# Branch B's scores as two split matmuls from stacked operands, with B's key block moved ahead of its query block, in a two-layer attention encoder

## The chip, the cores and the metric

One NeuronCore of one Trainium2 chip runs the whole program. The metric is the device time in microseconds (us) of one execution, lower is better. The engines that matter are TensorE (PE in the profile, its weight loads PEld), VectorE (DVE), ScalarE (ACT) and the DMA queues that SyncE (SP) and ACT issue on.

## The reference

Two layers over 512 tokens of width 1024. Each layer normalises x, projects it once, feeds four token mixers (A: windowed attention, B: differential attention, C: dilated, D: latent), gates and adds their outputs, projects, and runs a gated MLP. Branch B is the one changed most:

```python
def differential_attention(b_q, b_k, b_v, pos, q_norm, k_norm, ..., subln_g, lam_init):
    q = rms_norm(b_q.reshape(b, s, 2, B_HEADS, HEAD_DIM), q_norm)   # 2 maps x 4 heads x 64
    k = rms_norm(b_k.reshape(b, s, 2, B_HEADS, HEAD_DIM), k_norm)
    v = b_v.reshape(b, s, B_HEADS, B_V_DIM)                         # 4 heads x 128
    def block(args):                                                # 128 queries at a time
        sc = jnp.einsum('bqmhd,bsmhd->bmhqs', qblk, k) * scale
        sc = sc - slopes * dist
        a = jax.nn.softmax(sc, axis=-1)
        a = a[:, 0] - lam[None, :, None, None] * a[:, 1]            # two maps mixed
        return jnp.einsum('bhqs,bshv->bqhv', a, v)
```

## The kernel before

**Dense work.** Every projection is a series of "visits". A visit is six matmuls of 128x512 into one of PSUM banks 0 to 3: each fp32 operand is held as a rounded high part and a low part, and high x high, low x high and high x low are added up (`split3`, line 579). A weight tile comes by DMA into `raw`, ACT writes its high part `wh` (L961), DVE its low part `wl` (L1481, called "the split" below); one tile serves four visits.

**Order.** The engines' queues are written by generators that yield a due number, counted in visits; `together` merges them. So each engine has one fixed order, and semaphores do the rest. `ORDER` lists the dense blocks; `WINDOW` says over which visits the attention of a branch is spread. A window is cut into slots, one score each: B has 32 scores, 36 slots, over 45 visits (blocks br0a, gate0b, br0b and gate1a).

**A slot of B on TensorE.** A score is one matmul of `q_pad` (a head's 64 query rows, the other 64 rows zero) with `kT`, 512 keys, both plain fp32, into the single bank S1 (L859). DVE adds the distance bias while it copies the bank out (L2017), ACT takes the exponential (L1366). For every pair of scores (the two maps of a head) DVE mixes the two (L2007, L2009, L2011), TensorE transposes the mix (four matmuls on L614 into bank TA, "the turn"), ACT and DVE copy halves of it to SBUF (L1360, L2023), and TensorE multiplies it with the values (four matmuls, L850). The next score may not start before the bias has emptied S1 (`s_biased`). In its queue the mix of a pair stands ahead of the bias of the score after the pair, the turn stands one slot behind that, the values another two.

**Stacks of A.** Branch A already takes its scores from stacked operands: `q_two` holds query high parts over all 128 rows for a first matmul and low parts for a second, `kA` holds key high parts in 64 rows and key low parts in the other 64, and two matmuls of the rounded fp32 type (fp32r) make one score (L815). ACT writes the high parts (L1324), DVE copies them to the other 64 rows and subtracts for the low parts (L1955, L1957), for eight pieces of two halves each.

**Branch outputs.** Blocks br0a and br0b end in four merges on DVE each (L1621 and L1624), which multiply a bank by its gate and add it up. L1878 writes the low part of a turned tile of A's or D's output.

Of the kernel before, what the change touches and what calls it, by code (L numbers as in the profile page):

```python
# [13 lines left out]
F32 = mybir.dt.float32  # L14
F32R = mybir.dt.float32r
# [6 lines left out]
P = 128  # L22
# [87 lines left out]
class Own:  # L110
# [5 lines left out]
    def done(self, layer):  # L116
# [7 lines left out]
    nt_dve=24, ta_ready=128, ta_act=128, ta_dve=128, q_padded=48, q_hi=16, q_stacked=16, q_zeroed=2, s_ready=144, s_biased=144, p_ready=144, b_mixed=16, o_ready=128, o_out=24,  # L124
    gains_in=1, ssum=16, lam_dot=1, lam_exp=1, c_diff=2, c_exp=2, merged_sum=24, merged_hi=8, merged_lo=8, conv_mid=44,
    e_ready=22, hidden_val=22, hidden_hi=22, hidden_lo=22, act_step=189, dve_step=534, params_in=16, direct_in=8,
# [44 lines left out]
PADS = dict(C0=16, C1=8, C2=8, B=16)  # L171
# [31 lines left out]
def slots(name):  # L203

    begin, end, n = WINDOW[name]
    return [(step, begin + (end - begin) * step / (n + 4), (end - begin) / (n + 4)) for step in range(n + 4)]
# [24 lines left out]
def _build(nc, io, ctx):  # L231
# [20 lines left out]
    near = sb("near", [P, 2, NEAR])  # L252
    bias_b = sb("bias_b", [P, TT, SEQ])
    bias_c12 = sb("bias_c12", [P, 2, SEQ])
# [36 lines left out]
    q_two = stacked[:, AD + 4096:AD + 6144].rearrange("p (c h s n) -> p c h s n", c=4, h=2, s=2)  # L291
    gates = in_work(AD + 6144, 2048, t=4)
# [27 lines left out]
    c0_stats = nc.dram_tensor("c0_stats", (2, SEQ, 8), F32).ap()  # L320
    gate_keep = nc.dram_tensor("gate_keep", (2, P, 4 * SEQ), F32).ap()
# [31 lines left out]
    q_zeroed = signal("q_zeroed")  # L353
    s_ready = signal("s_ready")
# [35 lines left out]
    pad_clear = sem("pad_clear")  # L390

# [152 lines left out]
    def _(pe):  # L544
# [3 lines left out]
        def layer(l):  # L548
# [145 lines left out]
            def dense():  # L694
# [20 lines left out]
                for part in "qkv":  # L715
                    yield from block(f"B{part}", 4, tokens_out(H), pj_act)
# [28 lines left out]
            def turns():  # L745
# [26 lines left out]
                yield from head_turns(END["Aq"] + 6, chunks_of(stage))  # L772
                yield from head_turns(END["Bq"] + 6, chunks_of(stage))
                yield from head_turns(END["Bk"] + 6, chunks_of(stage))
# [51 lines left out]
            def attention_b(scores_of, begun):  # L826
# [5 lines left out]
                for step, at, pace in slots("B"):  # L832
                    yield at
                    if 3 <= step < n + 3 and step % 2 == 1:
                        pair = (step - 3) // 2
                        pe.wait_ge(*b_mixed.at(l, pair + 1))
                        pe.wait_ge(*ta_act.at(l, n_att[0]))
                        pe.wait_ge(*ta_dve.at(l, n_att[0]))
                        n_att[0] += 1
                        group[pair] = n_att[0]  # L840
                        transposed(TA, [mixed[:, pair % 2, P * k:P * k + P] for k in range(4)], ta_ready)
                    if 5 <= step < n + 5 and step % 2 == 1:
                        pair = (step - 5) // 2
# [7 lines left out]
                        last.then_inc(*o_ready.up())  # L851
                    if step < n:
# [3 lines left out]
                        pe.wait_ge(*q_padded.at(l, n_pad[0] + pads_of("B", step)))  # L856
                        pe.wait_ge(*s_biased.at(l, first + step))
                        for out, st, mv, start, stop in scores_of(step, S1):
                            mm(out, st, mv, start=start, stop=stop).then_inc(*s_ready.up())  # L859
# [11 lines left out]
            def attentions():  # L871
# [40 lines left out]
                yield from attention_b(b_scores, heads_in(B_HEADS, 96))  # L912
# [7 lines left out]
    def _(act):  # L920
# [47 lines left out]
        def layer(l):  # L968
# [107 lines left out]
            def dense():  # L1076
# [30 lines left out]
                n_dve[0] += 8  # L1107
                yield from staged_squares("Bq", 512)
                yield from staged_squares("Bk", 512)
                yield END["Bk"] + 2  # L1110
# [80 lines left out]
            def turns():  # L1191
# [49 lines left out]
                yield from q_out(END["Aq"] + 6, qA, 0)  # L1241
                yield from q_out(END["Bq"] + 6, qT, 4)
                yield from k_out(END["Bk"] + 6, kT, "bk")
# [42 lines left out]
            def pads():  # L1286
# [22 lines left out]
                def stacks_of_a():  # L1309
                    first, slot = done, slots("A")  # L1310
                    for piece in range(8):
# [9 lines left out]
                        for half in range(2):  # L1321
                            mine = slice(64 * half, 64 * half + 64)
# [18 lines left out]
                by_pair, by_map = (lambda g: slice(2 * g, 2 * g + 2)), (lambda g: slice(g, 4, 2))  # L1341
# [6 lines left out]
                yield from tiles_of("B", qT, B_HEADS, by_map)  # L1348

            def attention_b():  # L1350
# [3 lines left out]
                for step, at, pace in slots("B"):  # L1354
                    if 3 <= step < n + 3 and step % 2 == 1:
                        yield at + 0.05 * pace
                        pair = (step - 3) // 2
# [19 lines left out]
            def attentions():  # L1377
# [15 lines left out]
                yield from attention("C2", subs=4, mins=7, sums=10)  # L1393
                yield from attention("D", tile_at=0)
# [5 lines left out]
                act.dma_start(x_sb, keep).then_inc(*x_moved.up())  # L1400

# [6 lines left out]
    def _(dve):  # L1408
# [74 lines left out]
        def layer(l):  # L1483
# [220 lines left out]
            def dense():  # L1704
# [92 lines left out]
                yield from branch_out("br3b", 1, GATES, loaded=3)  # L1797
                yield from head_norm("Bq")
                yield from head_norm("Bk")
# [80 lines left out]
            def turns():  # L1880
# [42 lines left out]
                yield from q_out(END["Aq"] + 6, qA, 0)  # L1923
                yield from q_out(END["Bq"] + 6, qT, 4)
                yield from k_out(END["Bk"] + 6, kT, "bk")
# [18 lines left out]
            def stacks():  # L1944

                slot, n = slots("A"), 0
                for piece in range(8):
                    t, g = piece // 2, piece % 2
                    yield (slot[4 * piece - 4][1] + 0.8 * slot[0][2] if piece >= 2 else slot[0][1] - 6 + 1.5 * piece) + 0.3
                    for half in range(2):  # L1950
                        n += 1
# [6 lines left out]
                                        q_two[mine, 2 * g:2 * g + 2, half, 0, :].bitcast(F32), ALU.subtract).then_inc(*q_stacked.up(own))  # L1958

# [35 lines left out]
            def attention_b():  # L1995
# [3 lines left out]
                for step, at, pace in slots("B"):  # L1999
                    if 2 <= step < n + 2 and step % 2 == 0:  # L2000
                        yield at + 0.02 * pace
                        u = step - 2
# [9 lines left out]
                    if step < n:  # L2012
                        yield at + 0.2 * pace
                        dve.wait_ge(*s_ready.at(l, first + step + 1))
                        dve.wait_ge(*p_ready.at(l, first + step - 1))
                        dve.sem_inc(waits_met, 1)
                        v.tensor_tensor_reduce(out=scores[:, step % 2, :], in0=S1[:, :], in1=bias_b[:, step // 8, :], scale=B_SLOPES[(step % 8) // 2], scalar=MASKED, accum_out=stat[:, 5, step:step + 1], op0=ALU.add, op1=ALU.min).then_inc(*s_biased.up(own))  # L2017
                    if 3 <= step < n + 3 and step % 2 == 1:
                        yield at + 0.4 * pace
                        pair = (step - 3) // 2  # L2020
# [3 lines left out]
                    if step >= 11 and (step - 11) % 8 == 0:  # L2024
                        yield at + 0.6 * pace
                        t = (step - 11) // 8
# [7 lines left out]
            def attentions():  # L2034
# [42 lines left out]

                yield from attention("C0", biased_near(1, C_SLOPES[0], mins=12), keep_c0, 8, keys=near_keys)
# [7 lines left out]
            return norm1(), dense(), turns(), stacks(), attentions(), c_combine()  # L2086
# [31 lines left out]
```

## Time and profile before

| what | value |
|---|---|
| median of 3 runs (lowest, highest) | 2702.33 us (2701.27, 2704.14) |
| profiled execution, its time | 2702.53 us |
| its span, first to last instruction | 2700.7 us |
| PE busy | 2628.6 us (97%) |
| DVE busy | 1637.8 us (61%) |
| ACT busy | 1231.9 us (46%) |
| mean granted TensorE clock | 0.997 of 2.4 GHz |

The time of an execution is 1.8 us above its span. PE busy time is the union of matmul records whose ends are modelled, so what a matmul costs is read from the distance between starts. DVE's 61% is a mean over stages that differ a lot.

### The profile page before, as it was taken

To read this page: it belongs to the slowest core of one execution; us is meant where nothing else is said; L and a number is where in the kernel's file an instruction comes from. 1 tells how busy PE (TensorE), PEld (TensorE's weight loads), DVE (VectorE), ACT (ScalarE), POOL (GpSimd) and SP (SyncE) were. 2 spreads that over 40 slices of the span, in tenths; PEclk is the share of its full clock that TensorE was granted. 3 is DMA by queue.
4 is the path that set the end of the run, shared out by engine and by line. 5 is a ranking of instruction groups with operands and counts; after the bars stand their busy time and mean duration, and the time that the engine had idled before them with its cause. 6 is when DMAs were issued, how large, how long until landed. Compare 5 with 4: busy or idle time off the path is not lost. (4 is left out here: it accounts for less than half of the span.)

```text
span 2700.7 us, 36172 instructions
## 1 busy us (share of the span) xinstructions
PE 2628.6 (97%) x12982; PEld 2207.3 (82%) x12982; DVE 1637.8 (61%) x3432; ACT 1231.9 (46%) x2514; POOL 1.5 (0%) x6
## 2 busy tenths in 40 slices
PE   7999999999999999999999999999999999999999
PEld 6999987777877778888779998877788777888887
DVE  6554577545666647666664546775356666585665
ACT  5655554444544334333355455544446443343332
POOL 0000000000000000000000000000000000000000
PEclk9999999999999999999999999999999999999999
DMA  5212222222121323332342122221221213333332
GB/s 185 71 56 79 81 65 86 63 71 79 56 78 49 110 94 92 94 103 87 102 122 67 49 85 75 78 86 55 71 79 55 79 47 110 94 94 101 95 101 94
DMA packets 143874, 225.28 MB, mean 83 GB/s; under 512 B 15046, under 2 KB 69458, under 8 KB 142802
## 3 DMA queue, kind: packets, MB, share of 16 engines
q1 hardware_dynamic: 135842, 201.85, 25.1%
q10 hardware_dynamic: 7856, 21.12, 2.1%
q8 instruction: 106, 1.74, 0.3%
q14 instruction: 70, 0.57, 0.1%
HBM read 210.29 MB, written 12.65 MB: 83 GB/s over the span
## 5 line engine op out<-in xcount | busy, mean ns | idle before, releaser
L1481 DVE TENSOR_TENSOR s_wl<-s_raw,s_wh 128x1024 fp32r<-128x1024 f32 (+2 forms) x376 | 453.1, 1206 | 302.2 <-ACT s_wh L961 302.0
L961 ACT ACTIVATE s_wh<-s_raw 128x1024 fp32r<-128x1024 f32 (+2 forms) x376 | 392.0, 1042 | 398.3 <-PE bank L579 308.1
L579 PE MATMUL bank<-s_hTh,s_wh 128*128 128x512 f32 x1216 | 521.4, 429 | 1.6 <-DVE s_work L1839 1.4
L579 PE MATMUL bank<-s_hTh,s_wl 128*128 128x512 f32 x1216 | 475.5, 391 | 0.0
L579 PE MATMUL bank<-s_hTl,s_wh 128*128 128x512 f32 x1216 | 474.4, 390 | 0.0
L579 PE MATMUL bank<-s_wh,s_hTh 128*128 128x512 f32 (+1 forms) x1088 | 458.3, 421 | 4.2 <-DVE s_early L1621 3.3
L579 PE MATMUL bank<-s_wh,s_hTl 128*128 128x512 f32 (+1 forms) x1088 | 426.0, 392 | 0.0
L579 PE MATMUL bank<-s_wl,s_hTh 128*128 128x512 f32 (+1 forms) x1088 | 425.5, 391 | 0.0
L579 PEld LDWEIGHTS bank<-s_hTh,s_wh 128*128 128x128 f32 x1216 | 228.9, 188 | 70.0 <-issue 24.3
L1278 ACT ACTIVATE s_work<-s_work,s_stat 128x128 f32<-128x128 f32 (+3 forms) x320 | 167.5, 524 | 257.8 <-DVE s_work L2053 113.6
L579 PEld LDWEIGHTS bank<-s_hTl,s_wh 128*128 128x128 f32 x1216 | 229.2, 189 | 66.5 <-issue 24.4
L579 PEld LDWEIGHTS bank<-s_wh,s_hTh 128*128 128x128 f32 x1088 | 251.7, 231 | 34.2 <-issue 4.0
L579 PEld LDWEIGHTS bank<-s_wh,s_hTl 128*128 128x128 f32 x1088 | 251.6, 231 | 26.8
L579 PEld LDWEIGHTS bank<-s_wl,s_hTh 128*128 128x128 f32 x1088 | 253.5, 233 | 22.6 <-issue 0.5
L579 PEld LDWEIGHTS bank<-s_hTh,s_wl 128*128 128x128 f32 x1216 | 228.7, 188 | 49.3
L614 PE MATMUL bank<-s_consts,s_work 128*128 128x128 f32 (+1 forms) x1432 | 216.4, 273 | 15.3 <-DVE s_gTl L1878 7.5
L614 PEld LDWEIGHTS bank<-s_consts,s_work 128*128 128x128 f32 (+1 forms) x1432 | 172.7, 139 | 70.6 <-issue 31.2
L1978 DVE COPY s_work<-bank 128x128 f32<-128x128 f32 (+1 forms) x224 | 77.3, 345 | 207.6 <-PE bank L614 98.2
L579 PE MATMUL bank<-s_wh,s_gTh 128*128 128x512 f32 (+1 forms) x432 | 167.3, 387 | 5.7 <-ACT s_work L990 5.2
L579 PE MATMUL bank<-s_wh,s_gTl 128*128 128x512 f32 (+1 forms) x432 | 166.3, 385 | 0.0
L579 PE MATMUL bank<-s_wl,s_gTh 128*128 128x512 f32 (+1 forms) x432 | 166.1, 385 | 0.0
L579 PE MATMUL bank<-s_gTh,s_wh 128*128 128x512 f32 x256 | 111.3, 435 | 5.9 <-DVE s_gTl L1878 3.0
(202 smaller groups left out, 3409.5 us busy)
## 6 DMA issues: line engine op xcount, KB each, us to landing
s_raw<-in_w_in SPq DMA_DIRECT2D x168, 512.0 KB, 3.6
s_raw<-in_ffn_w_up SPq DMA_DIRECT2D x176, 256.0 KB, 3.1
s_raw<-in_ffn_w_down SPq DMA_DIRECT2D x44, 512.0 KB, 3.7
s_raw<-in_w_branch SPq DMA_DIRECT2D x32, 512.0 KB, 3.7
s_raw<-in_w_o SPq DMA_DIRECT2D x16, 512.0 KB, 3.8
x_keep<-s_work ACTq DMA_DIRECT2D x2, 2048.0 KB, 11.3
s_raw<-in_w_in SPq DMA_DIRECT2D x16, 256.0 KB, 2.9
gate_keep<-s_early ACTq DMA_DIRECT2D x4, 1024.0 KB, 4.3
```

Source lines behind the costliest of these rows:

```text
L579: last = mm(PJ[b][:, 0:width], st, mv, start=i == 0 and n == 1, stop=i == ntiles - 1 and n == 3 * chunks)
L614: last = nc.tensor.transpose(dst[0:m, (at + n) * P:(at + n) * P + k], src, ident[0:k, 0:k])
L961: a(wh[:, k % 3, 0:n], raw[:, s, 0:n], ACT.Copy).then_inc(*hi_split.up(own))
L1278: a(probs[:, u % 2, x0:x0 + w], scores[:, u % 2, x0:x0 + w], ACT.Exp, scale=-1.0, bias=stat[:, mins, c:c + 1], accum_out=stat[:, sums, c:c ...
L1481: v.tensor_tensor(wl[:, k % 3, 0:n], raw[:, k % 2, 0:n], wh[:, k % 3, 0:n].bitcast(F32), ALU.subtract).then_inc(*tile_split.up(own))
L1978: v.tensor_copy(probsT[:, u % 2, P * mid:P * hi], src[:, P * mid:P * hi]).then_inc(*ta_dve.up(own))
```

## The change

Four things, in both layers. (1) A score of B is two fp32r matmuls: `q_four` holds query parts, `kB` key parts, stacked as for A. (2) The key block Bk stands ahead of the query block Bq; its turns come during A's attention (slots 21 to 25.5), and ACT and DVE each write two 64-row halves of each turned key tile. (3) B has 37 slots instead of 36 over the same visits; the mix of a pair stands behind the bias of the score after next, turn and values one slot later, values ahead of the turn. (4) The two halves of a query piece of A are written in different slots. One half of B's keys lies over a table of mask and bias that is needed again in layer 2, so the table is stored to HBM and loaded back once.

```diff
-     ("br3a", 8), ("br3b", 8), ("Bq", 16), ("Bk", 16), ("Bv", 16), ("br0a", 8), ...
+     ("br3a", 8), ("br3b", 8), ("Bk", 16), ("Bq", 16), ("Bv", 16), ("br0a", 8), ...
@@ slots
+    count = n + (5 if name == "B" else 4)
+KEY_SLOTS = (21, 22.5, 24, 25.5)
@@ tiles
+    kB = [... for t in (stacked[:, AD + 2048:AD + 4096], tables[:, NEAR:NEAR + 2048])]
+    q_four = [... for t in (stacked[:, 6144:7168], stacked[:, AD + 14336:AD + 15360])]
@@ TensorE, attention_b
-                    if 3 <= step < n + 3 and step % 2 == 1:
-                        pair = (step - 3) // 2
-                        ... the turn
-                    if 5 <= step < n + 5 and step % 2 == 1:
-                        pair = (step - 5) // 2
+                    if 6 <= step < n + 6 and step % 2 == 0:
+                        pair = (step - 6) // 2
...
+                    if 4 <= step < n + 4 and step % 2 == 0:
+                        pair = (step - 4) // 2
+                        ... the turn
@@ TensorE, b_scores
-                    return [(out[:], q_pad[:, n // 2, n % 2, :], kT[:, n // 2, :], True, True)]
+                    c = n // 2
+                    return [(out[:], q_four[c % 2][:, c // 2, n % 2, part, :], kB[n % 2][:, c, :], part == 0, part == 1) for part in range(2)]
@@ ScalarE, key turns (in place of k_out for Bk) and stacks
+                for t in range(4):
+                    behind = 0.5 if KEY_SLOTS[t] % 1 == 0 else 0.1
+                    yield slot_of("A", KEY_SLOTS[t] + behind)
+                    src = group()
+                    for half in range(2):
...
+                        a(kB[half][mine, :, P * t:P * t + P], src[mine, :].rearrange("p (c n) -> p c n", c=4), ACT.Copy,
+                          scale=prm[mine, ROW["bk"]:ROW["bk"] + 1]).then_inc(*(td_act if half else k_half).up(own))
+                def stacks_of_b():
...
+                        for half in range(2):
+                            if half and piece >= 2:
+                                yield slot[4 * piece - 3][1] + 0.8 * slot[0][2]
+                            a(q_four[g][mine, :, half, 0, :], qT[mine, g:4:2, P * t:P * t + P], ACT.Copy).then_inc(*q_hi.up(own))
-                yield from tiles_of("B", qT, B_HEADS, by_map)
+                yield from stacks_of_b()
@@ ScalarE, table out and in (first layer only)
+                    act.dma_start(near_keep, near[:, 1, :]).then_inc(tables_moved, 16)
+                    act.dma_start(bias_keep, bias_c12[:]).then_inc(tables_moved, 16)
...
+                    act.dma_start(near[:, 1, :], near_keep).then_inc(tables_moved, 16)
+                    act.dma_start(bias_c12[:], bias_keep).then_inc(tables_moved, 16)
@@ VectorE, key turns
+                        v.scalar_tensor_tensor(kB[half][other, :, P * t:P * t + P], TD[mine, :]..., prm[mine, ...],
+                                               kB[half][mine, :, P * t:P * t + P].bitcast(F32), ALU.mult, ALU.subtract)
@@ VectorE, stacks of A: one half per slot
-                    yield (slot[4 * piece - 4][1] + 0.8 * slot[0][2] if piece >= 2 else slot[0][1] - 6 + 1.5 * piece) + 0.3
                     for half in range(2):
+                        yield slot[4 * piece - 3 + half][1] + 0.6 * slot[0][2] if piece >= 2 else slot[0][1] - 5.7 + 1.5 * piece
@@ VectorE, new: stacks_b
+                        v.tensor_copy(q_four[g][other, :, half, 0, :], q_four[g][mine, :, half, 0, :].bitcast(F32))
...
+                        v.tensor_tensor(q_four[g][mine, :, half, 1, :], qT[mine, g:4:2, P * t:P * t + P],
+                                        q_four[g][mine, :, half, 0, :].bitcast(F32), ALU.subtract)
@@ VectorE, attention_b
-                    if 2 <= step < n + 2 and step % 2 == 0:
-                        yield at + 0.02 * pace
-                        u = step - 2
-                        ... the mix, ahead of this slot's bias
...
+                        yield at + 0.45 * pace
+                        u = step - 3
+                        ... the mix, behind this slot's bias (odd slots)
```

TensorE's queue at the second pair of B, before. `s_consts,s_work` is the turn, `s_work` alone the values, `s_work,s_q_pad` a score; the L579 rows are one visit (its six matmuls are three kinds, twice), other visits are left out:

```order
L859 MATMUL bank<-s_work,s_q_pad 128x512
...
L614 MATMUL bank<-s_consts,s_work 128x128 x4
L850 MATMUL bank<-s_work 128x128 x4
L859 MATMUL bank<-s_work,s_q_pad 128x512
L579 MATMUL bank<-s_hTh,s_wh 128x512
L579 MATMUL bank<-s_hTl,s_wh 128x512
L579 MATMUL bank<-s_hTh,s_wl 128x512
```

And in the changed kernel, where L631 is the turn, L861 the values and L878 a score:

```order
L878 MATMUL bank<-s_stacked 128x512 x2
L596 MATMUL bank<-s_hTh,s_wh 128x512
L596 MATMUL bank<-s_hTl,s_wh 128x512
L596 MATMUL bank<-s_hTh,s_wl 128x512
...
L861 MATMUL bank<-s_work 128x128 x4
L631 MATMUL bank<-s_consts,s_work 128x128 x4
L878 MATMUL bank<-s_tables,s_stacked 128x512 x2
```

Each score is two matmuls, and the values now stand between the visit and the turn. With one visit after the odd score, the turn follows that score by one visit and the values.

VectorE's queue from B's third score on, before (the four ISA rows are biases with their accumulator reads, L1481 the split, L1621 and L1624 a merge, L2007 to L2011 the mix):

```order
L2007 RECIPROCAL s_stat<-s_stat 128x1
L2009 SCALAR_TENSOR_TENSOR s_stat<-s_stat,s_lam 128x1
L2011 SCALAR_TENSOR_TENSOR s_work<-s_work,s_stat 128x512
L2017 ISA s_work,s_stat<-bank,s_bias_b 128x512
...
L2017 ISA s_work,s_stat<-bank,s_bias_b 128x512
L2017 ISA s_stat 128x1
L1481 TENSOR_TENSOR s_wl<-s_raw,s_wh 128x1024
L2023 COPY s_work<-bank 128x256
L1621 SCALAR_TENSOR_TENSOR s_work<-s_work,bank 128x512
L1624 TENSOR_TENSOR s_work<-s_work 128x512
```

And in the changed kernel, a little later, between the second mix (L2106 to L2110) and the third one (L2098 is the bias, L2048 and L2050 a stack half, L1687 and L1690 a merge, L2116 the copy, L1547 the split):

```order
L2048 CAST s_stacked<-s_stacked 64x2x128
L2050 TENSOR_TENSOR s_stacked<-s_work,s_stacked 64x2x128
L1687 SCALAR_TENSOR_TENSOR s_work<-s_work,bank 128x512
L1690 TENSOR_TENSOR s_work<-s_work 128x512
L2098 ISA s_work,s_stat<-bank,s_bias_b 128x512
...
L2116 COPY s_work<-bank 128x256
...
L1547 TENSOR_TENSOR s_wl<-s_raw,s_wh 128x1024
L2098 ISA s_work,s_stat<-bank,s_bias_b 128x512
L2098 ISA s_stat 128x1
L2106 RECIPROCAL s_stat<-s_stat 128x1
```

A second stack half stands between the copy and the split. The mix, which used to stand ahead of the even slot's bias, now stands behind the odd slot's bias, directly ahead of the turn that waits for it.

## Rows read from the trace of the kernel before

**Rows 1.** The page: busy us of each engine and its share of the span.

```profile
PE 2628.6 (97%) x12982; PEld 2207.3 (82%) x12982; DVE 1637.8 (61%) x3432; ACT 1231.9 (46%) x2514; POOL 1.5 (0%) x6
```

**Rows 2.** Windows A, B, A of layer 2: length, PE, PEld, DVE, ACT busy, clock.

```profile
641.60:779.30 137.70, 131.05 (x738) 111.62 (x736) 87.40 (x220) 72.54 (x194) 0.00 (x0) 1.00 0.26 79
779.30:896.50 117.20, 116.33 (x545) 86.45 (x546) 75.11 (x168) 53.37 (x115) 0.00 (x0) 1.00 0.21 57
...
1982.70:2121.90 139.20, 132.59 (x738) 112.87 (x737) 87.50 (x220) 72.77 (x194) 0.00 (x0) 0.99 0.26 78
```

**Rows 3.** Waits of TensorE inside B's window, layer 1: us, times, longest.

```profile
PE bank L614 <- DVE s_work L2011: 0.4, 1, 0.4
PE bank L859 <- DVE s_stat L2017: 0.2, 1, 0.2
```

**Rows 4.** Timeline of one B score: start us, us, engine line op.

```profile
839.45 1.02 PE L859 MATMUL bank<-s_work,s_q_pad 128*128 128x512 f32 x2
...
840.54 0.39 PE L579 MATMUL bank<-s_gTl,s_wh 128*128 128x512 f32 x1
840.77 0.40 PE L579 MATMUL bank<-s_gTh,s_wl 128*128 128x512 f32 x1
```

**Rows 5.** Timeline of a turn and the values in B.

```profile
841.69 0.60 PE L614 MATMUL bank<-s_consts,s_work 128*128 128x128 f32 x4
...
842.13 1.06 PE L850 MATMUL bank<-s_work 128*128 128x128 f32 x8
...
843.02 1.02 PE L859 MATMUL bank<-s_work,s_q_pad 128*128 128x512 f32 x2
```

**Rows 6.** Timeline of a stacked score of A, 384 keys.

```profile
670.50 0.60 PE L815 MATMUL bank<-s_stacked 128*128 128x384 f32 x2
670.94 0.40 PE L579 MATMUL bank<-s_gTh,s_wh 128*128 128x512 f32 x1
```

**Rows 7.** From a stacked score of A, 256 keys, to its bias.

```profile
666.85 0.48 PE L815 MATMUL bank<-s_stacked 128*128 128x256 f32 x2
...
667.55 0.48 DVE L2042 CUSTOM_DVE_ANT_0 s_work<-bank,s_near,s_sink 128x256 f32<-128x256 f32 x1 [0.21 <-PE bank L815]
```

**Rows 8.** Timeline of DVE in B's first slots.

```profile
791.15 1.22 DVE L1481 TENSOR_TENSOR s_wl<-s_raw,s_wh 128x1024 fp32r<-128x1024 f32 x1
792.29 0.42 DVE L2023 COPY s_work<-bank 128x256 f32<-128x256 f32 x1
...
794.14 0.16 DVE L2007 RECIPROCAL s_stat<-s_stat 128x1 f32<-128x1 f32 x1
...
795.26 0.68 DVE L2017 CUSTOM_DVE_ANT_0 s_work<-bank,s_bias_b 128x512 f32<-128x512 f32 x1
...
795.87 0.68 DVE L1621 SCALAR_TENSOR_TENSOR s_work<-s_work,bank 128x512 f32<-128x512 f32 x1
...
797.19 0.68 DVE L1621 SCALAR_TENSOR_TENSOR s_work<-s_work,bank 128x512 f32<-128x512 f32 x1
```

**Rows 9.** Timeline: a mix and the turn that waited for it.

```profile
847.55 0.16 DVE L2007 RECIPROCAL s_stat<-s_stat 128x1 f32<-128x1 f32 x1
...
848.81 0.45 PEld L614 LDWEIGHTS bank<-s_consts,s_work 128*128 128x128 f32 x4 [0.18 <-DVE s_work L2011]
```

**Rows 10.** Groups of instructions of A's window, by form: stack halves; a two-operand operation from PSUM.

```profile
L1957 DVE TENSOR_TENSOR s_stacked<-s_work,s_stacked 64x256 fp32r<-64x256 f32 x12 | 5.0, 419 | 0.4
L1955 DVE CAST s_stacked<-s_stacked 64x256 fp32r<-64x256 f32 x12 | 3.5, 289 | 4.8 <-ACT s_stacked L1324 3.8
L1878 DVE SCALAR_TENSOR_TENSOR s_gTl<-bank,s_gTh 128x512 fp32r<-128x512 f32 x4 | 2.8, 692 | 5.9 <-ACT s_gTh L1189 5.4 <-DVE s_stat L1501 0.5
```

**Rows 11.** TensorE's waits in A's window of layer 1.

```profile
PE bank L614 <- DVE s_work L1978: 0.9, 1, 0.9
PE bank L815 <- DVE s_stat L2042: 0.9, 1, 0.9
```

**Rows 12.** DMA issues of large tiles: KB each, us to landing.

```profile
x_keep<-s_work ACTq DMA_DIRECT2D x2, 2048.0 KB, 11.3
```

More of the change, by code:

```diff
@@ L1241, in turns @@
                 yield from q_out(END["Aq"] + 6, qA, 0)
+                for t in range(4):
+                    behind = 0.5 if KEY_SLOTS[t] % 1 == 0 else 0.1
+                    yield slot_of("A", KEY_SLOTS[t] + behind)
+                    src = group()
+                    for half in range(2):
+                        if half:
+                            yield slot_of("A", KEY_SLOTS[t] + behind + 0.25)
+                        mine = slice(64 * half, 64 * half + 64)
+                        if l == 0 and t == 0 and half == 1:
+                            act.wait_ge(tables_moved, 16 * 2)
+                        act.wait_ge(*own.done(l))
+                        a(kB[half][mine, :, P * t:P * t + P], src[mine, :].rearrange("p (c n) -> p c n", c=4), ACT.Copy,
+                          scale=prm[mine, ROW["bk"]:ROW["bk"] + 1]).then_inc(*(td_act if half else k_half).up(own))
                 yield from q_out(END["Bq"] + 6, qT, 4)
-                yield from k_out(END["Bk"] + 6, kT, "bk")
                 for t in range(4):
@@ L1923, in turns @@
                 yield from q_out(END["Aq"] + 6, qA, 0)
+                for t in range(4):
+                    behind = 0.75 if KEY_SLOTS[t] % 1 == 0 else 0.35
+                    for half in range(2):
+                        yield slot_of("A", KEY_SLOTS[t] + behind + 0.6 * half)
+                        if half == 0:
+                            n_turn[0] += 1
+                            turn = n_turn[0]
+                        mine, other = slice(64 * half, 64 * half + 64), slice(64 - 64 * half, 128 - 64 * half)
+                        dve.wait_ge(*(td_act.at(l, turn) if half else k_half.at(l, t + 1)))
+                        dve.wait_ge(*own.done(l))
+                        v.scalar_tensor_tensor(kB[half][other, :, P * t:P * t + P], TD[mine, :].rearrange("p (c n) -> p c n", c=4), prm[mine, ROW["bk"]:ROW["bk"] + 1],
+                                               kB[half][mine, :, P * t:P * t + P].bitcast(F32), ALU.mult, ALU.subtract).then_inc(*(td_dve if half else dve_step).up(own))
                 yield from q_out(END["Bq"] + 6, qT, 4)
-                yield from k_out(END["Bk"] + 6, kT, "bk")
                 begin = B_NORM
@@ L2011, in attention_b @@
                         v.scalar_tensor_tensor(mixed[:, u // 2 % 2, :], p1, share, p0, ALU.mult, ALU.add).then_inc(*b_mixed.up(own))
[L2012 to L2018, printed above, removed]
+                    if 4 <= step < n + 4 and step % 2 == 0:
                         yield at + 0.4 * pace
-                        pair = (step - 3) // 2
+                        pair = (step - 4) // 2
                         src = att_group()
```

110 lines of the change are left out of this document (84 added, 26 removed), and 2 rows, old and new, of the table ORDER.

## Prediction

> **What bounds the kernel now.** I read the page first: TensorE is busy 97% of the span, DVE 61%, ACT 46% [rows 1]. Then the windows over the stretches that the change touches. In B's window of layer 1 TensorE is busy 116.33 of 117.20 us and DVE 75.11 of them; A's window shows 131.05 of 137.70 [rows 2]. TensorE's list of waits has 0.6 us inside B's window [rows 3]. So time goes away where TensorE gets less to do, as long as nobody makes it wait. The reader should also see what that list does not say: DVE, at 64% of B's window, is the second engine, and it works through one fixed queue. How much room it has is settled slot by slot, in the timelines.
>
> **What the scores give back.** A plain fp32 score starts at 839.45; the second fp32r matmul behind it starts at 840.54 and the third at 840.77 [rows 4]. A dense matmul takes 0.23, so the score holds TensorE for 840.54 - 839.45 - 0.23 = 0.86 us. A stacked score of B does not occur in the trace. Its nearest row is one of A: two matmuls over 384 keys take 0.44 us up to the next dense start [rows 6], which was 670.94 - 670.50; at 0.23 per 512 columns, 128 more columns twice add 0.11, so 0.55. That row stands behind fp32 work. Behind a dense visit I take two dense matmuls, 0.46. Half of the scores stand behind a turn, half behind a visit: (0.86 - 0.55) x 32 + (0.86 - 0.46) x 32 = 9.9 + 12.8 = 22.7 us over both layers. Bounds: 0.55 everywhere gives 19.8, 0.46 everywhere 25.6.
>
> The Trainium skill has a rule on this price, in "FP8 and Floating Point Precision", section TensorE Precision Notes: a true fp32 product takes four passes through the array. The trace agrees nearly, 0.86 us against 0.23 [rows 4]. By the rule two passes of four would go, 0.43 us a score or 27.5 us in all, against the 22.7 from the rows.
>
> **What DVE then does to TensorE.** This is the term that decides. I work it out in B's new order. TensorE's pieces: turn 0.44, values 0.89 [rows 5], visit six times 0.23 = 1.37, score 0.55 or 0.46. DVE's pieces, from start to next start: split 1.14, copy 0.42, bias 0.61, merge 1.32 [rows 8], mix 1.12 [rows 8]; a stack half 0.29 + 0.42 = 0.71 [rows 10]. From a mix's start to the turn it releases: 848.81 - 847.55 = 1.26 [rows 9]. From a score's start to its bias: 0.70 with 256 keys [rows 7]; with 512 two matmuls are longer by 0.115 each, so 0.92 behind a turn and 0.84 behind a visit.
>
> A pair of slots is turn, score, visit, score, visit, values on TensorE: 0.44 + 0.55 + 1.37 + 0.46 + 1.37 + 0.89 = 5.1 us, or 6.4 when it holds a third visit. In the same pair DVE does bias, copy, bias, mix = 2.8 us, two stack halves in three pairs of four, 1.4 us, and a split (one for four visits) or merges on top. The order is what counts. Before, the mix stood ahead of the even slot's bias and the turn a slot behind it. Now turn and mix are neighbours: the last odd score, its bias (0.84 + 0.61) and the mix (1.26) take 2.7 us up to the turn, and TensorE has 0.46 + 1.37 + 0.89 = 2.7 for it. There is no slack, and whatever else stands between is a wait.
>
> One pair in full, the third (its DVE order is in the section on the change). Let its turn start at 0; DVE has been free since -0.14. Stack half to 0.6, merge to 1.9, bias to 2.5. The odd score could start at 0.44 + 0.55 + 1.37 = 2.36 but waits for that bias until 2.75: 0.4. Copy to 2.9, stack half to 3.6, split to 4.8, bias to 5.4, mix: next turn at 6.7. TensorE is there at 2.75 + 0.46 + 1.37 + 0.89 = 5.5 and waits 1.2. The same for every pair of a layer: up to the first turn 2.0 (a split stands between bias and mix, and there are no values yet); second pair 1.4 (three merges); third 1.6; the following pairs, under gates without merges, 0, 0.1, 0.1, 0.1, 0.6 (split without third visit), 0, 0.3; the merges of br0b 1.2, 0.7, 0.5; the rest 0.4. Sum 9.0 us a layer. The 0.6 us of today are in it, so 8.4 are new, 16.8 over both layers. This is the term that I know least: half of it if DVE gets ahead in the pairs with three visits more than I grant, 1.4 times if ACT (53.37 us of work in the window [rows 2], with its own fixed queue) is late with high parts or probabilities too. So 8 to 24.
>
> **A's window.** The stack pieces that are pulled apart stand in front of two waits, 0.9 and 0.9 us per layer [rows 11]; with 0.7 us of DVE instead of 1.4 in one piece I give both back: 3.6 us over both layers at most, 0 at least. The key turns cost: eight operations of 64x512 per layer with two operands, priced by the 692 ns of the nearest one [rows 10], and as much on ACT, where the old k_out wrote quarter-size pieces. They share bank TD, so turn 3 waits until DVE has written both halves of turn 2, behind a bias and a split; that is some 0.5 to 1 us at two turns. DVE is busy 87.40 of 137.70 us here [rows 2], so 1 to 4 us over both layers. The two cancel within what I can tell: 0, from -3 to +4.
>
> **Hidden.** Swapping Bk and Bq moves equal visits. The stack pieces for B's first scores (ACT four copies, DVE two pieces of 1.4 us) lie behind A's last slots; the second one is ahead of the low part of A's last tile, for which br0a waits anyway; I add 0.3 a layer, 0.6. The table: 0.6 + 0.5 MB out behind C and back behind B, in the first layer. The nearest row is 2 MB in 11.3 us [rows 12], so some 6 us of transfer each way, issued by ACT, whose queue goes on. SP's weight loads share the engines at a share of 0.21 [rows 2]; the load back stands behind the 2 MB residual, which is needed a full 45 us later. Zero, or 2 if a weight tile comes late.
>
> **Sum.** -22.7 + 16.8 + 0 + 0.6 = -5.3. The profiled execution took 2702.53, 0.2 above the median of the runs, so both give 2697.2. Three quarters of what TensorE saves come back as waits for DVE's mix and bias.
>
> **Rivals.**
> 1. *The scores' time is kept.* DVE's queue has idle time (75.11 of 117.20 us busy [rows 2]; with 12 halves of 0.71 about 84 of 105), and the waits come to a third: 22.7 - 6 = -17, 2685.5; with none at all, 2680. Against it speak the third pair's 6.9 us of DVE work in 5.1 us of TensorE's. Chance 0.27.
> 2. *Slower.* The same mechanism, stronger: the mix behind the odd bias. It decides when the new waits of a layer exceed 22.7 / 2 = 11.4 us, against the 8.4 forecast; each pair costing 0.3 us more (16 pairs) is enough for half of that, ACT's delay for the rest. With 14 us a layer: +5.3, 2708. Chance 0.15.
> 3. *The table's transfers* delay weight tiles in layer 1 by two or three us on top of the forecast: 2700. Chance 0.05.
> 4. *The clock.* A's window of layer 2 had a granted clock of 0.99 where the others had 1.00 [rows 2]: one short stretch at the lower level of 1.2 GHz. The missing 0.01 of 139.20 us is 1.4 us of clock. If waits of 1 to 2 us in a row bring one more such stretch in each layer: +2.8, 2700. The Trainium skill, "TensorE: Matmul & The Clock Gate", section What's actually happening, says that the low clock is the default and activity lifts it, which speaks for this rival; the trace shows 1.00 in B's window. Chance 0.03.
>
> The forecast has 0.50.
>
> **How the numbers follow.** A change under 0.2% (5.4 us) can't be told from none. The forecast runs from about -12 to 0 and is split by that line: 0.24 of its 0.50 is faster, the rest same. Rival 1 is all faster, 0.27. Rival 2 has 0.13 slower and 0.02 same; rivals 3 and 4 are same, but for 0.02. With waits of 8 to 24 and the scores' bounds of 19.8 to 25.6 the sum runs from -17 to +5; rival 1 extends the low side. Range 2682 to 2708, the forecast's own 2690 to 2703. Faster 0.51, same 0.34, slower 0.15.
>
> **What the next profile will show.** Scores of B as two matmuls with some 0.5 us between their start and the next dense start. B's window of 48 visits at 114 to 115 us, instead of 117.2 (105 if rival 1 is right, over 118 if rival 2). In the list of waits the turn L631 waiting for the mix L2110, 10 times or more and 5 to 8 us a layer, and the score L878 for its bias, 1 to 2 us; the longest ones at the window's start and in br0b. DVE over 73% busy there. In A's window the waits for L2042 and L1978 gone, one or two for the key halves L2000 new. What would make me wrong: waits on the mix of under 3 us a layer, or waits on ACT's lines.

## The result and the profile after

| kernel | median us | ratio to the kernel before, 95% interval |
|---|---|---|
| before, same chip (13 runs) | 2702.36 | |
| after (13 runs) | 2707.38 | 1.0016, 1.0009 to 1.0023 |

The change costs 4 to 5 us (5.0 by the medians, 4.3 by the ratio). 2697.2 was forecast, a gain of 5.3: the direction is wrong. The slowdown is small, but its interval lies clear of one. All comparisons in this document are of undisturbed runs.

The page of the kernel after, busy us of each engine, beside [rows 1]:

```profile
span 2706.2 us, 36324 instructions
PE 2610.7 (96%) x12982; PEld 2212.7 (82%) x12982; DVE 1671.6 (62%) x3504; ACT 1246.2 (46%) x2530; POOL 1.5 (0%) x6
```

TensorE's busy time is 17.9 us shorter, and the span is 5.5 us longer: 23 us of new idle time have come in. The windows of the same work, A's (layer 1) and B's (both layers), beside [rows 2]; columns are length, PE, PEld, DVE, ACT busy, POOL, clock, DMA share, GB/s:

```profile
639.90:783.20 143.30, 132.79 (x743) 112.67 (x742) 94.95 (x233) 80.70 (x208) 0.00 (x0) 1.00 0.26 78
783.20:898.80 115.60, 106.90 (x543) 88.50 (x544) 84.30 (x193) 52.96 (x111) 0.00 (x0) 0.99 0.20 57
2127.40:2243.20 115.80, 106.02 (x540) 87.82 (x541) 84.09 (x192) 53.20 (x113) 0.00 (x0) 0.99 0.19 54
```

B's window is 1.6 us shorter, A's 5.6 us longer: the loss is in A's window, where I had put zero. TensorE's waits there (us in total, times, longest), beside [rows 11], and then inside B's window, beside [rows 3]:

```profile
PE bank L631 <- DVE s_tables L2000: 5.3, 3, 2.2
PE bank L822 <- DVE s_work L2168: 3.5, 3, 1.5
PE bank L834 <- DVE s_stat L2135: 0.5, 1, 0.5
```

```profile
PE bank L631 <- DVE s_work L2110: 7.2, 6, 2.2
PE bank L596 <- DVE s_gTl L1944: 1.5, 1, 1.5
PE bank L878 <- DVE s_stat L2098: 0.7, 2, 0.4
```

L631 is a turn. In A it waits for L2000, DVE's half of a key tile; in B for L2110, the mix. (The 1.5 us on L1944 stand at the window's entry, and are no part of the sums below.)

Where the span went, from the start of one dense block to the start of the next, both layers of before and after (us):

| stretch | before | after | change, both layers |
|---|---|---|---|
| br3b, A's first slots | 17.0, 18.5 | 15.6, 15.6 | -4.4 |
| first block of B (equal visits) | 34.9, 34.9 | 35.0, 35.0 | +0.1 |
| second block of B, to Bv (called the key block below): the key turns | 37.8, 37.8 | 43.3, 43.3 | +11.0 |
| Bv | 34.2, 34.1 | 34.5, 34.5 | +0.7 |
| B's window, br0a to gate1b | 117.2, 117.1 | 115.6, 115.8 | -2.9 |
| everything else | | | +1.0 |

Why the key turn waits is one piece of the timeline of the kernel after (start us, us, engine, line, operation):

```profile
725.30 0.68 ACT L1274 ACTIVATE s_stacked<-bank,s_prm 64x512 fp32r<-64x512 f32 x1
726.02 0.74 DVE L2000 SCALAR_TENSOR_TENSOR s_stacked<-bank,s_prm,s_stacked 64x512 fp32r<-64x512 f32 x1 [0.89 <-ACT s_stacked L1274]
726.08 0.68 ACT L1274 ACTIVATE s_tables<-bank,s_prm 64x512 fp32r<-64x512 f32 x1
...
727.71 0.29 DVE L2071 COPY s_work<-bank 128x128 f32<-128x128 f32 x1 [0.94 <-ACT s_work L1299]
727.92 0.62 DVE L2135 CUSTOM_DVE_ANT_0 s_work<-bank,s_near,s_sink 128x384 f32<-128x384 f32 x1
...
728.66 0.76 DVE L2000 SCALAR_TENSOR_TENSOR s_tables<-bank,s_prm,s_tables 64x512 fp32r<-64x512 f32 x1
...
729.56 0.63 PE L631 MATMUL bank<-s_consts,s_work 128*128 128x128 f32 x4 [2.19 <-DVE s_tables L2000]
```

ACT has delivered its second half at 726.76 (726.08 + 0.68), and DVE stands idle until 727.71. But the next thing in DVE's queue is the copy L2071, which waits for ACT, and then the bias L2135; the second key half comes behind both, at 728.66 instead of 726.8. The bank is free only then, and the next turn waits 2.19 us.

### The profile page after: what moved, and what is told of

Its sections match the earlier page's. It is cut to its first block and busy times, and to the rows that moved or that the text cites. A ratio compares the mean times of both kernels' runs of the same rounds, so it can differ in the third digit from the quotient of the medians.

```text
span 2706.2 us, 36324 instructions
## 1 busy us (share of the span) xinstructions
PE 2610.7 (96%) x12982; PEld 2212.7 (82%) x12982; DVE 1671.6 (62%) x3504; ACT 1246.2 (46%) x2530; POOL 1.5 (0%) x6
## 5 line engine op out<-in xcount | busy, mean ns | idle before, releaser
L1547 DVE TENSOR_TENSOR s_wl<-s_raw,s_wh 128x1024 fp32r<-128x1024 f32 (+2 forms) x376 | 453.3, 1206 | 302.0 <-ACT s_wh L982 301.5
L596 PE MATMUL bank<-s_hTh,s_wh 128*128 128x512 f32 x1216 | 504.0, 414 | 1.5 <-DVE s_work L1905 1.4
L631 PE MATMUL bank<-s_consts,s_work 128*128 128x128 f32 (+1 forms) x1432 | 218.0, 274 | 37.8 <-DVE s_work L2110 14.9
L631 PEld LDWEIGHTS bank<-s_consts,s_work 128*128 128x128 f32 (+1 forms) x1432 | 171.1, 139 | 92.5 <-issue 40.0
L2071 DVE COPY s_work<-bank 128x128 f32<-128x128 f32 (+1 forms) x224 | 77.5, 346 | 221.4 <-PE bank L631 93.6
L1299 ACT ACTIVATE s_work<-bank 128x256 f32<-128x256 f32 (+1 forms) x224 | 78.1, 349 | 84.7 <-PE bank L631 83.5
```

The lines of the kernel that those rows point to most:

```text
L596: last = mm(PJ[b][:, 0:width], st, mv, start=i == 0 and n == 1, stop=i == ntiles - 1 and n == 3 * chunks)
L631: last = nc.tensor.transpose(dst[0:m, (at + n) * P:(at + n) * P + k], src, ident[0:k, 0:k])
L1299: a(probsT[:, u % 2, P * lo:P * mid], src[:, P * lo:P * mid], ACT.Copy).then_inc(*ta_act.up(own))
L1547: v.tensor_tensor(wl[:, k % 3, 0:n], raw[:, k % 2, 0:n], wh[:, k % 3, 0:n].bitcast(F32), ALU.subtract).then_inc(*tile_split.up(own))
L2071: v.tensor_copy(probsT[:, u % 2, P * mid:P * hi], src[:, P * mid:P * hi]).then_inc(*ta_dve.up(own))
```

## The experiments

All times are beside runs of the kernel before on the same chip: 2701.28 (first four), 2701.2 (next four), 2702.1 (last two). The blocks are those of the table above. Two theories stood: **theory 1**, the order of DVE's queue makes the waits; **theory 2**, DVE's load does, and the order only decides who waits.

**1. The mix ahead of the odd bias** (after, B's window).

```diff
+                    if 3 <= step < n + 3 and step % 2 == 1:
+                        yield at + 0.02 * pace
+                        ... # mix, L2106 to L2110
                     if step < n:
                         yield at + 0.2 * pace
                         ... # bias
-                    if 3 <= step < n + 3 and step % 2 == 1:
-                        yield at + 0.45 * pace
-                        ... # mix
```

> After, with one edit: in B's window VectorE's three mixing instructions stand ahead of the odd slot's bias instead of behind it. Theory 1 (the turn's waits for the mix, 14.9 us over both layers, come from VectorE's order: the mix stands behind a bias that waits for a score): the mix starts about a bias earlier, so most of those waits go; what stays is where two evictions of the stack piece stand ahead as well, about 4 to 6 us. The bias of the odd slot comes 1.2 us later, and a score waits for it at a few places, 2 to 3 us in place of today's 1.5. Time 6 to 9 us under after, about 2699 to 2701. Theory 2 (VectorE has too much to do in these stretches, and the order only decides who waits): the waits for the mix go over into waits of the scores for the bias, and the time is within 2 us of after.

Measured: 2692.64 us, ratio 0.9964 (0.9951 to 0.9976); by the ratios 14 us under after, more than either theory said. TensorE's longest waits in B's window of layer 1 and the windows of both layers:

```profile
PE bank L878 <- DVE s_stat L2110: 3.6, 3, 1.9
PE bank L596 <- DVE s_gTl L1944: 1.5, 1, 1.5
```

```profile
782.80:891.70 108.90, 104.96 (x543) 88.47 (x544) 83.39 (x193) 52.23 (x111) 0.00 (x0) 0.98 0.21 60
2119.40:2228.10 108.70, 104.10 (x544) 87.27 (x545) 83.61 (x193) 51.95 (x111) 0.00 (x0) 1.00 0.21 61
```

(In this kernel L2110 is the bias and L2104 the mix.) In layer 1 no turn waits for the mix any more; in layer 2 one does, for 0.7 us. The scores' waits for the bias grew from 0.7 to 3.6 us a layer, so a part did move over, as theory 2 said, but of 16.2 us of waits over both layers 8.3 are gone. That is theory 1's 6 to 9. DVE does the same work, 83.4 us, now in 108.9: a load of 77%. Load alone does not make the waits of B.

The two windows are 13.8 us shorter together. 8.3 are waits, some 3.5 the low clock that after has in both layers (see run 2), and 2 have no term. The 0.98 of layer 1 here costs next to nothing: layer 1 of run 3, with B's queues the same and the clock at 1.00, took 108.8.

**2. The second key half ahead of the next bias** (after, A's window).

```diff
-                        yield slot_of("A", KEY_SLOTS[t] + behind + 0.6 * half)
+                        yield slot_of("A", KEY_SLOTS[t] + behind + 0.2 * half)
```

> After, with one edit: in A's window VectorE's second half of each key tile stands ahead of the next slot's bias instead of behind it. Theory 1 (the later key turns wait 10.5 us over both layers for the second half because it stands in VectorE's queue behind a copy and a bias, and the bias behind a score): the waits for the second half fall to under 2 us, the bias behind it is 0.8 us later and costs a score under 1 us a time where it has no slack; the stretch ahead of Bv falls by 3 to 5 us a layer from 43.3, and the time is 5 to 9 us under after, 2698 to 2702. Theory 2 (the loss is the added work of VectorE and the turns in slots that had none to spare): the waits go to the scores for the bias, and the time stays within 2 us of after.

Measured: 2705.97 us, ratio 1.0012 (1.0004 to 1.0021), only 1 us under after. The key block did what theory 1 said, 39.4 and 39.4 us against 43.3 and 43.3. But Bv behind it grew from 34.5 to 36.0 and 39.0 us. Bv in both layers:

```profile
745.50:781.50 36.00, 31.63 (x178) 26.39 (x176) 26.37 (x71) 22.83 (x60) 0.00 (x0) 1.00 0.30 100
2086.30:2125.30 39.00, 34.27 (x178) 28.71 (x176) 27.07 (x71) 23.54 (x61) 0.00 (x0) 0.91 0.30 93
```

TensorE's waits in Bv are 2.9 us in layer 1 and 3.2 in layer 2, so most of the 3 us between the two is the clock. Over both blocks layer 1 gained 2.3 us (75.5 against 77.8) and layer 2 lost 0.6 (78.4).

B's window was not touched in this kernel, and it shows by chance what the clock does:

```profile
781.50:895.40 113.90, 105.40 (x544) 87.48 (x545) 84.37 (x192) 52.70 (x111) 0.00 (x0) 1.00 0.20 58
2125.30:2241.10 115.80, 106.99 (x544) 88.74 (x545) 84.38 (x192) 52.69 (x111) 0.00 (x0) 0.99 0.20 57
```

The waits are nearly equal (7.3 and 7.6 us on the mix, 0.7 and 0.7 on the bias), the lengths differ by 1.9 us, and so does the granted clock. 0.3 of the 1.9 is a longer first wait. After has the low clock in both layers.

**3. Both edits**, the two diffs above together.

> After, with both edits: the mix ahead of the odd slot's bias in B's window and the second key half ahead of the next bias in A's. Theory 1: the two savings add, 11 to 17 us under after, so 2690 to 2696, and under the kernel before as well. Theory 2: within 3 us of after, 2704 to 2708.

Measured: 2692.38 us, ratio 0.9962 (0.995 to 0.9975). That lies in theory 1's range, but the savings did not add: it is no more than with the mix alone. The key block and Bv of both layers:

```profile
705.50:745.00 39.50, 36.83 (x216) 31.37 (x215) 29.11 (x71) 24.72 (x59) 0.00 (x0) 1.00 0.17 44
745.00:782.50 37.50, 33.14 (x178) 27.62 (x176) 26.52 (x71) 23.11 (x60) 0.00 (x0) 0.95 0.29 95
2041.90:2081.30 39.40, 36.73 (x216) 31.32 (x215) 28.77 (x71) 24.34 (x58) 0.00 (x0) 1.00 0.15 43
2081.30:2120.20 38.90, 34.16 (x177) 28.65 (x176) 27.04 (x71) 23.51 (x61) 0.00 (x0) 0.91 0.29 93
```

The waits for the key halves fell to 0.8 us (from 5.3), and Bv lost 3.0 and 4.4 us: two waits, and behind them a stretch at the low clock (0.95 and 0.91). Layer 1 of run 2 has the same two waits at 1.00 and took 36.0. So the waits cost 1.5 us more than after's, and the clock 1.5 in layer 1 and up to 2.9 in layer 2. Two rows of the waits of A's window, layer 1:

```profile
PE bank L822 <- ACT s_work L1299: 1.9, 1, 1.9
...
PE bank L631 <- DVE s_work L2071: 0.9, 1, 0.9
```

```profile
748.49 0.57 ACT L1009 ACTIVATE s_work<-bank 128x512 f32<-128x512 f32 x1
748.97 0.58 ACT L1011 ACTIVATE s_work<-bank 128x512 f32<-128x512 f32 x1
749.44 0.27 ACT L1299 ACTIVATE s_work<-bank 128x128 f32<-128x128 f32 x1
...
749.74 0.52 PE L822 MATMUL bank<-s_work 128*128 128x64 f32 x3 [1.95 <-ACT s_work L1299]
```

ACT's copy L1299, for which the values wait, stands behind two evictions of Bq. But these values waited before too: 1.5 us in after (the longest wait on L2168), and in the kernel before, in a row that [rows 11] does not show:

```profile
PE bank L803 <- ACT s_work L1266: 1.3, 1, 1.3
```

So ACT adds 0.4 us to an old wait. New are 0.9 us on the copy L2071 and 0.5 on a bias. In layer 1 that is together some 1.9 of the 4.5 us that the key halves gave, and the clock took 1.5; in layer 2 the clock took more than the waits had left. Theory 1 holds for the key halves. Of what was lost again, about half went to other waits, as theory 2 said, and the rest to the low clock.

**4. The halves apart, alone** (before, with part four of the change only). On ACT, and likewise on DVE:

```diff
                         for half in range(2):
+                            if half and piece >= 2:
+                                yield slot[4 * piece - 3][1] + 0.8 * slot[0][2]
```

> Before, with part four of the change alone: in A's window the two halves of a query tile's stack are evicted one slot apart on ScalarE and VectorE. It tells what of A's window is worth what: if the halves apart give back the waits for the stack and for the scores' buffer as forecast, 2 to 3.6 us under before (2699 to 2700.5), and the key turns alone then cost 13 to 15 us over both layers; if they give nothing (the trace of after shows 0.9 and 0.4 us less at each of a few waits), within 1.5 us of before, and the key turns cost 11.

Measured: 2697.04 us, ratio 0.9982 (0.9973 to 0.9991), 4.2 us faster. br3b 15.6 and 15.6, the key block's place 37.4 and 37.6, B's window unchanged. So this part is worth a little more than its upper bound of 3.6. Some of it, about 1.5 us, is the stretch of low clock in layer 2 of [rows 2] that went: br3b took 18.5 us there against 17.0 in layer 1. After's key blocks are 11.6 us longer than these two, so the key turns cost the whole 11.

**5. The turn a slot later, alone** (before, with part three only; scores plain fp32, no stack pieces). On DVE, with turn, values and ACT's piece each a slot later too:

```diff
-                    if 2 <= step < n + 2 and step % 2 == 0:
-                        yield at + 0.02 * pace       # mix, ahead of the bias
+                    if 3 <= step < n + 3 and step % 2 == 1:
+                        yield at + 0.45 * pace       # mix, behind the bias
```

> Before, with part three of the change alone: in B's window the turn and the values stand a slot later and the mix behind the odd slot's bias; the scores stay plain fp32, and VectorE has no stack pieces. It tells the part of the waits that the place makes from the part that the shorter score makes. If the place alone makes them (theory 1 pure), the turn waits 6 to 8 us a layer for the mix as in after, and the time is 12 to 16 us over before, about 2714 to 2718. If place and density together do it, the pair now has 0.7 us more of TensorE's work and 1.4 us less of VectorE's in three pairs of four, and the waits are 2 to 4 us a layer: 2705 to 2709. If density alone does it, it stays within 2 us of before.

Measured: 2713.15 us, ratio 1.0041 (1.0027 to 1.0055), 12 us slower. B's window 122.5 and 122.6 against 117.2 and 117.1. The waits for the mix in layer 1:

```profile
PE bank L615 <- DVE s_work L2018: 4.8, 3, 2.1
```

That is between my cases: the place alone, in a sparser window with DVE at 62% (76.40 of 122.50 us), makes three of the six waits on the mix, and 4.8 of their 7.2 us.

**6. The old slots with the new scores** (after, with part three undone; on DVE the diff of run 5 backwards, the turn one slot behind the mix).

> After, with part three of the change undone: the scores of B stay stacked, but the mix stands ahead of the even slot's bias, the turn one slot behind it, and the values two slots behind the turn, as before. Theory 1 (the place of the mix behind the bias makes the waits): B's window falls from 115.6 to 108 to 110 us as with the mix ahead of the odd bias (108.9), so the time is about 2691 to 2695, and the slot's delay brings nothing of its own. Theory 2 (the stacked scores need the delay, since otherwise the mix delays the bias of the even slot): scores wait for their bias 3 us a layer more than the 3.6 with the mix ahead, and the time is 2697 to 2702.

Measured: 2701.0 us, ratio 0.9998 (0.999 to 1.0007). B's window 113.4 and 113.7: 2.1 to 2.2 under after, but 4.5 and 5.0 over run 1. The delay by a slot, which I expected to be worth nothing, is worth 4.5 to 5.0 us a layer, once the mix isn't behind the bias. The waits of layer 1:

```profile
PE bank L631 <- DVE s_work L2104: 7.0, 9, 1.6
...
PE bank L878 <- DVE s_stat L2110: 1.1, 2, 0.6
```

That is 8.1 us, no less than after's 7.9; what these windows gain on after is about what the clock costs there (1.00 here, 0.99 in after). The time lies in theory 2's range, but the scores' waits for the bias that it named are only 1.1 us. With the old slots the mix belongs to the score just before it, and waits for its exponential (from the timeline of this kernel):

```profile
810.20 0.16 DVE L2100 RECIPROCAL s_stat<-s_stat 128x1 f32<-128x1 f32 x1 [0.55 <-ACT s_work L1424]
```

**7 to 10. Where the key turns stand.** One line each, on top of run 3 (7, 8, 9) or of run 1 (10):

```diff
-KEY_SLOTS = (21, 22.5, 24, 25.5)
+KEY_SLOTS = (20, 21.5, 23, 24.5)   # run 7
+KEY_SLOTS = (20, 22, 24, 26)       # run 8
+KEY_SLOTS = (21, 23, 24.5, 26)     # runs 9 and 10
```

> Both edits (mix ahead of the odd bias, second key half ahead of the next bias), and the four key turns a slot earlier, at 20, 21.5, 23 and 24.5. With the key half ahead the values behind A's slot 26 wait 1.9 us for ScalarE (its copy stands behind the last key half and two evictions of Bq), and a low-clock stretch follows. If that wait comes from the last key turn standing next to Bq's last evictions, it goes, and the time is 3 to 5 us under the version with both edits (2692.4), 2687 to 2690. If it comes from ScalarE's evictions alone, the time stays within 1.5 us of it.

> Both edits, and the four key turns two slots apart, at 20, 22, 24 and 26. If what is left of the key turns' cost is the work crowded into few slots, the waits for the key halves fall to zero, and the time is 2 to 4 us under the version with both edits; the last turn, now at slot 26 beside Bq's last evictions, may hold a wait of 1.5 to 2 us for ScalarE, which would leave 2691 to 2693.

> Both edits (mix ahead of the odd bias, second key half ahead of the next bias), and the key turns at slots 21, 23, 24.5 and 26: the first stays where it is, since one slot earlier it waited 3.0 us for VectorE's normalisation, and the others have two, one and a half and one and a half slots between them. If what both edits left of the key turns' cost (5.0 us in the first layer, 6.3 in the second, over the two blocks that held 72.0 before) comes from crowding, these blocks fall to 74 to 75 us and the time is 2686 to 2689. If it is the same evictions wherever they stand, since ScalarE is then late for the last slots, the blocks stay at 77 to 78 and the time at 2691 to 2694.

> The same spacing of the key turns, 21, 23, 24.5 and 26, with the mix ahead but the second key half behind the next bias, as in after. The second half of the first tile has a slot more before the next turn wants its bank: its wait of 2.2 us goes, the two others (1.8 and 1.3 us) stay, 2 us a layer less than with the mix ahead alone: about 2688 to 2690. If crowding is not what it hangs on, the time stays at 2691 to 2694.

| run | median us | ratio (interval) | key block + Bv, layer 1, 2 |
|---|---|---|---|
| before | | | 72.0, 71.9 |
| after | 2707.38 | 1.0016 (1.0009, 1.0023) | 77.8, 77.8 |
| 1 mix ahead | 2692.64 | 0.9964 (0.9951, 0.9976) | 77.8, 77.8 |
| 3 both | 2692.38 | 0.9962 (0.995, 0.9975) | 77.0, 78.3 |
| 7 keys a slot earlier | 2700.37 | 0.9994 (0.9985, 1.0003) | 79.9, 82.1 |
| 8 two apart, from 20 | 2696.07 | 0.9979 (0.997, 0.9988) | 80.7, 81.1 |
| 9 from 21 to 26, both | 2691.12 | 0.9956 (0.9944, 0.9969) | 76.2, 76.2 |
| 10 from 21 to 26, mix ahead | 2691.56 | 0.996 (0.9946, 0.9973) | 76.6, 76.5 |

Runs 7 and 8 missed: slot 20 is too early, and both show a new wait of 3.0 us in each layer for the normalisation of the block that is to be turned:

```profile
PE bank L631 <- DVE s_work L1605: 3.0, 1, 3.0
```

In run 8 the waits for the key halves themselves fell to 1.0 us, in one place.

Runs 9 and 10 gain 1.2 to 1.6 us a layer over run 1 in these blocks, less than expected if crowding were all of it. Run 10 missed its time, and its reason too: the wait of 2.2 us that was to go is still there, and the key halves make 5.6 us of waits in four places, where after has 5.3 in three. In the time runs 9 and 10 cannot be told from runs 1 and 3, for the intervals overlap, but all four are about 10 us faster than the kernel before. In run 9 the clock was 1.00 in both blocks, and 4.2 us a layer stay over before: real waits, 6.4 us in layer 1 against 2.8. The largest, 1.7 us, is the values' wait in Bv that before has too, at 1.3. The new ones are 2.7 us on the key halves, in three places, and 0.7 on the copy.

## Why the prediction was wrong

**The scores: right.** Forecast 0.55 us behind a turn and 0.46 behind a visit. The timeline of the kernel after:

```profile
812.99 0.70 PE L878 MATMUL bank<-s_stacked 128*128 128x512 f32 x2
...
826.66 0.63 PE L878 MATMUL bank<-s_stacked 128*128 128x512 f32 x2
827.12 0.39 PE L596 MATMUL bank<-s_hTh,s_wh 128*128 128x512 f32 x1
```

827.12 - 826.66 = 0.46, the median of 18 such pairs in the window; behind turns the median of 14 is 0.54. So 11.35 us a layer are saved. Run 6, with the clock at 1.00, closes the sum: 117.2 - 0.6 (old waits) - 11.35 + 8.1 (new ones) = 113.35, measured 113.4. Run 1 gives 108.85 against 108.9 in layer 1, but 109.45 against 108.7 in layer 2, so the sum holds to within 0.8 us.

**The waits of the turn in B: right in place and size.** Forecast 9.0 us a layer; the trace shows 7.9 in layer 1 (7.2 on the mix, 0.7 on the bias) and 8.3 in layer 2. They are fewer and longer than I said: six on the mix and not ten or more, and 0.7 us for the bias and not 1 to 2. The pairs, forecast against measured: first turn 2.0 and 2.17, second 1.4 and 1.36, third 0.4 + 1.2 and 0.36 + 1.29, the two long ones in br0b 1.2 and 1.75, 0.7 and 0.44. The third turn and its cause, in the kernel after:

```profile
809.38 1.23 DVE L1547 TENSOR_TENSOR s_wl<-s_raw,s_wh 128x1024 fp32r<-128x1024 f32 x1
...
810.52 0.68 DVE L2098 CUSTOM_DVE_ANT_0 s_work<-bank,s_bias_b 128x512 f32<-128x512 f32 x1
...
811.32 0.16 DVE L2106 RECIPROCAL s_stat<-s_stat 128x1 f32<-128x1 f32 x1
...
812.58 0.66 PE L631 MATMUL bank<-s_consts,s_work 128*128 128x128 f32 x4 [1.29 <-DVE s_work L2110]
```

Split, bias, mix, turn, in that order, as forecast. (The forecast's step from the end of the third pair's bias at 2.5 to its score at 2.75 has no row; its wait was 0.4 forecast and 0.36 measured. And from the median, 2702.33, the sum of -5.3 gives 2697.0, not 2697.2.) The Trainium skill, "Perfetto Trace Analysis", section Per-engine timelines, says that DVE and ACT are strict FIFO; the trace agrees: nothing passes in front, even where the engine stands idle for 0.94 us (the copy at 727.71).

**The clock: a rival at 0.03 that came.** Behind the first turn's wait in layer 1 dense matmuls stand 0.43 us apart instead of 0.23 for 3.0 us, the level of 1.2 GHz:

```profile
796.89 0.54 PE L596 MATMUL bank<-s_gTh,s_wh 128*128 128x512 f32 x1
797.23 0.63 PE L596 MATMUL bank<-s_gTl,s_wh 128*128 128x512 f32 x1
797.65 0.63 PE L596 MATMUL bank<-s_gTh,s_wl 128*128 128x512 f32 x1
```

Run 2 prices it: 113.9 us without and 115.8 with it, so 1.6 to 1.9 us a layer; the rival said 1.4. It is why B's window was 115.6 and 115.8 and not the forecast 114 to 115, with fewer waits than forecast. The scores and waits gave -22.7 + 15 us (waits of 16.2 over both layers, less 1.2 of today), the clock +3.5, and 1.3 stay unassigned: the -2.9 of the table. The Trainium skill's rule in "TensorE: Matmul & The Clock Gate", section What's actually happening, that the low clock is the default and activity lifts it, was cited for this rival, and I gave it too little: a wait of 2 us was followed by one in after and in run 3. It is no fixed toll. The same wait in run 2, layer 1, brought none, and of the 18 B windows of after and the runs that hold a wait of about 2 us (1.9 to 2.5), 8 hold a stretch of low clock. And where the mix stands ahead it costs little: layer 1 took 108.9 us with it in run 1, 108.8 without in run 3. Why one wait brings it and the next does not stays open.

**A's window: the step that failed.** "So 1 to 4 us over both layers" for the key turns; they cost 11.0 in their block. The work itself was counted rightly (eight halves of 0.74 to 0.76 us on DVE, eight of 0.68 on ACT, instead of 128x128 pieces of 0.35). What I had not done is what I did for B: write out the queue. I had named the wait ("turn 3 waits until DVE has written both halves of turn 2, behind a bias and a split") and put 0.5 to 1 us on two turns; it was 2.2, 1.7 and 1.3 on three, every turn but the first. The evictions were priced by their busy time, and what stands in front of the second half without the copy's wait for ACT ahead of the bias. And with "the two cancel" I set a term that had been worked out (the halves apart, 3.6, measured 4.2 alone, some of it clock) against one that had been guessed. The corrected sum, against the spans: -5.3 forecast, +6.6 for A's window (11.0 - 4.4 in place of 0), +3.5 for the clock in B, -1.8 for B's waits (15.0 instead of 16.8), +2.5 that no term claims (1.3 in B's window, 1.0 elsewhere, 0.2 in the other blocks of the table) = +5.5, as measured. The 1.0 elsewhere holds more low clock too, in blocks that the change leaves alone: from 1363 to 1420 us the granted clock is 0.97 in after and 1.00 in before.

**What was right otherwise.** Bv, with the stack pieces for B's first scores: +0.3 a layer, as forecast. The transfers of the tables show in no block of the first layer. In A the wait for L1978 of [rows 11] has gone; the one for L2042, now L2135, is down from 0.9 to 0.5 us, not gone. DVE is busy 73% of B's window (84.30 of 115.60).

**What was not run.** Why 4.2 us a layer remain in run 9 isn't settled. DVE does 8.6 us more in these two blocks than before (55.7 against 47.1), ACT 8.5 more (47.8 against 39.3); whether the key tiles in smaller pieces on both engines, as before, would remove it was not tried.

## What to carry to other kernels

When a step is moved beside the step that feeds it, look at what stands between them in the feeder's queue, and move the feeder first: the same change with one block of code in another order is 0.36% faster than before in place of 0.16% slower. Write the queue out for every place where the change puts an operation on the path, not only for the one that looks dangerous; "they cancel" is no estimate. And after each edit look at the next block too: of the 3.9 us that run 2 won in one block, the next lost 1.5 to waits in layer 1, and 4.5 to waits and the low clock in layer 2.

## What the runs showed of the hardware

A TensorE wait of 2 us can cost up to nearly twice itself, when a stretch of low clock follows it: in after a wait of 2.17 us was followed by dense matmuls 0.43 us apart for 3.0 us, and in Bv of layer 1 the same waits took 36.0 us at a clock of 1.00 (run 2) and 37.5 at 0.95 (run 3). It follows in 8 of 18 windows of B with such a wait, and in none of the six windows of before, run 4 and run 6, whose longest wait is 1.6. And the busy share of DVE does not tell what it costs TensorE: at 77% of a window (run 1) it made 3.6 us of waits in layer 1, at 73% (after) 7.9, and at 62% (run 5) 4.8.
